# A float32 decoder trunk on one core: W-times-x products as three 256-column matmuls per tile instead of one of 512 and one of 256

## The chip, the cores and the metric

The kernel runs on one NeuronCore of a Trainium2 chip (trn2). The metric is the device time of one execution in microseconds (us), as a median over runs. TensorE (PE in the profile) does the matmuls; its weight loads are shown as an engine of their own, PEld. VectorE is DVE, ScalarE is ACT, GpSimd is POOL, and SyncE (SP) issues most DMAs.

## The reference

The reference is a two-layer decoder trunk on x of 256 tokens by 2048 channels, in float32. Layer 0 mixes retention (4 heads) with a gated linear recurrence; layer 1 is 16-head causal attention with a bias table. Each layer ends in a gated MLP with a width-3 depthwise convolution. Cut to the parts that load weights:

```python
def reference(x, ...):
    for l in range(2):
        hn = rmsnorm(x, norm_mix[l])
        y = even_mixer(hn, ev_w_in[0], ...) if l % 2 == 0 else odd_mixer(hn, od_w_in[0], ...)
        x = x + y                            # both mixers: (hn @ w_in) -> mix -> @ w_out
        x = x + conv_ffn(rmsnorm(x, norm_ffn[l]), ffn_w_up[l], ..., ffn_w_down[l])
    return x

def conv_ffn(h, w_up, conv_w, conv_b, w_down):       # w_up 2048 x 11264, w_down 5632 x 2048
    u = causal_dwconv(h @ w_up, conv_w, conv_b)
    gate, val = jnp.split(u, 2, axis=-1)
    return (jax.nn.gelu(gate) * val) @ w_down
```

## The kernel before

**Split operands.** TensorE reads its operands as fp32r. To keep float32 accuracy, each weight chunk W is split into w_hi (a rounded copy, made by ACT) and w_lo = W - w_hi (made by DVE), and each activation x is split in the same way; the tiles `xs` and `act` hold x_hi and x_lo side by side, 256 tokens each, so that one tile is 512 columns. A product is w_hi x_hi + w_hi x_lo + w_lo x_hi; the term w_lo x_lo is left out.

**Chunks.** Weights stream in chunks of 256 rows by 512 columns (512 KB) into a ring of four slots: SP issues the DMA into `raw`, ACT makes w_hi (`split`, L373), DVE makes w_lo (`split`, L958), and PE uses the chunk. A slot is written again when the semaphore `chunk_used` says that PE is through with it. Each of the three engines walks through the same list of chunks: 12 blocks of 8 chunks for the input projection, 4 blocks of 8 for w_out, 22 half-pairs of 8 for w_up, 4 blocks of 22 for w_down, and the same for layer 1. In between, at fixed chunks of a block (`stage` 0 to 7), ACT and DVE do the work on the previous block's result.

**Products with W loaded.** `chunk_products` (L660) takes two k-tiles (u) by four output tiles (m) of a chunk, so 8 tiles of 128 x 128 weights. For each it runs `hi`, 512 columns wide (w_hi against x_hi and x_lo at once, L675), and `lo`, 256 columns wide (w_lo against x_hi, L679). Two tiles are interleaved: hi, hi, lo, lo. An output tile has a PSUM bank of 512 columns: columns 0:256 hold w_hi x_hi + w_lo x_hi, and columns 256:512 hold w_hi x_lo, the cross half. Four banks make a group, and blocks alternate between the two groups. The last chunk of the program, `last_chunk` (L692), has the same matmuls with the m loop outside, and a signal for each m.

**Draining.** One engine operation can't add the two halves out of PSUM, so ACT first copies the cross half to the SBUF tile `cross` (`copy_cross`, L384), DVE adds the main half to it (`drain_normed`, L974), and multiplies by `rstd` (L976), with the semaphores `cross_copied`, `acc_drained` and `normed` between them. For w_out and w_down, DVE adds `cross` and then the main half to the residual x_res (`add_residual`, L990 and L992). At the end of the program DVE does the same, tile by tile, straight from PSUM (L1450, L1452), and SP stores each tile. Two blocks of layer 0 (5 and 8) use the same group as the block before them; they are drained in two halves (`HALVED`).

**Products with x loaded.** The v blocks of layer 0 and all input blocks of layer 1 load x as the stationary operand and stream W, in `chunk_values` (L708): three matmuls of 512 columns one after another into one bank. They are not touched by the change.

Of the kernel before, what the change touches and what calls it, by code (L numbers as in the profile page):

```python
# [85 lines left out]
class Phase:  # L86


    def __init__(self, layer):
# [10 lines left out]
        own_in = 10 if layer == 0 else 0  # L100
        self.cross_in = layer * (10 + OUTB + 2 * PAIRS + OUTB)
        self.cross_out = self.cross_in + own_in
        self.cross_up = self.cross_out + OUTB
        self.cross_down = self.cross_up + 2 * PAIRS
        self.normed_in = layer * (10 + 2 * PAIRS)
        self.normed_up = self.normed_in + own_in
# [21 lines left out]
def build(nc, x_t, params, w_gates, rope, decay, rel_bias, buckets, identity,  # L128
# [21 lines left out]
    cross, _ = place("cross", [P, BT, S])  # L150
# [64 lines left out]
    cross_copied, acc_drained, normed = sem("cross_copied"), sem("acc_drained"), sem("normed")  # L215
    cross_half, half_drained = sem("cross_half"), sem("half_drained")
# [139 lines left out]
    def _(eng):  # L356
# [18 lines left out]
        def copy_cross(n, used, group, halved=False):  # L375

            eng.wait_ge(chunk_used, used)
            if not (isinstance(n, int) and n == 0):
                eng.wait_ge(acc_drained, n)
            if halved:  # L380
                act_f(cross[:, 0:2, :], ps[:, 4 * group:4 * group + 2, S:2 * S], ACT.Copy).then_inc(cross_half, 1)
                act_f(cross[:, 2:4, :], ps[:, 4 * group + 2:4 * group + 4, S:2 * S], ACT.Copy).then_inc(cross_copied, 1)
            else:
                act_f(cross[:, :, :], ps[:, 4 * group:4 * group + 4, S:2 * S], ACT.Copy).then_inc(cross_copied, 1)  # L384

# [19 lines left out]
        def residual(stage, j, n, used, group, norm):  # L405
            if stage == 2:
                copy_cross(n, used, group)
# [8 lines left out]
        def mlp_post(stage, ph, half, j):  # L416
# [3 lines left out]
            if stage == 2:  # L420
                copy_cross(n, chunk_end(ph.q_up + 4 * j + 2 * half, KC - 1), half)
            if stage == 3:
                eng.wait_ge(normed, ph.normed_up + 2 * j + half + 1)
# [22 lines left out]
        def lru_conv_first(half):  # L446
            eng.wait_ge(normed, half + 1)
# [34 lines left out]
        def gelu_branch(half):  # L482
            eng.wait_ge(normed, 3 + half)
            act_f(gl_gelu[:, half * BT:(half + 1) * BT, :], h[:, :, :], ACT.Gelu_apprx_tanh).then_inc(gelu_gl, 1)

        def silu_gate(grp):
            eng.wait_ge(normed, (7, 10)[grp])
# [51 lines left out]
        def even_post(b, stage):  # L539

            ph = phases[0]
            if b and stage == drain_stage(EVEN_GROUPS, b) and EVEN_BLOCKS[b - 1][0] != "v":
# [966 lines left out]
```

## Time and profile before

| | us |
|---|---|
| median of 3 runs | 2249.24 (2248.87 to 2251.79) |
| the profiled execution, its own time | 2249.13 |
| its span in the trace | 2247.3 |
| PE busy | 2240.0 |
| PE weight loads busy | 1943.2 |
| DVE busy | 1494.7 |
| ACT busy | 1157.5 |

The span runs from the first to the last instruction of the core. "Busy" is the time covered by at least one instruction of the engine. Matmuls overlap each other, so the mean length of one (396 ns for 512 columns) is not what it costs in a stream; that is read from one start to the next. A row of a timeline that ends in "x2" merges two instructions, and its time is that of the first one's start.

### The profile page before, as it was taken

The numbers are of one execution on the slowest core, as the hardware profiler recorded it, in microseconds if no ns is written. First come the engines' busy times: TensorE is split into PE (matmuls) and PEld (weight loads), VectorE is DVE, ScalarE is ACT, GpSimd is POOL, SyncE is SP. The second block draws the span as 40 slices with busy tenths as digits, with TensorE's granted clock in tenths as the row PEclk, the third lists the DMA queues.
The fourth block names the chain that finished last, engine by engine and source line by source line (L and its number), as shares of the span: only waits on it lengthen the run. The fifth ranks groups of instructions, "written<-read, shape, count | busy, mean of one in ns | idle before, by whom it ended". The sixth has DMA issues, their size and how long they took to land.

```text
span 2247.3 us, 34057 instructions
## 1 busy us (share of the span) xinstructions
PE 2240.0 (100%) x12502; PEld 1943.2 (86%) x12502; DVE 1494.7 (67%) x1798; ACT 1157.5 (52%) x1451; POOL 7.2 (0%) x17
## 2 busy tenths in 40 slices
PE   9999999999999999999999999999999999999999
PEld 8888888888888888888888888888888888888888
DVE  7886766777677777544565656567777777774444
ACT  6654355555555555444455555555555555553333
POOL 0000000000000000000000000000000000000000
PEclk9999999999999999999999999999999999999999
DMA  8655655666666666666675555556665666566664
GB/s 273 182 178 164 192 176 184 185 189 190 189 188 187 196 179 193 189 185 192 197 224 169 167 180 168 169 179 188 187 197 178 192 187 197 178 196 200 200 187 143
DMA packets 216385, 420.90 MB, mean 187 GB/s; under 512 B 13061, under 2 KB 13589, under 8 KB 216176
## 3 DMA queue, kind: packets, MB, share of 16 engines
q1 hardware_dynamic: 214416, 413.59, 59.9%
q0 software_dynamic: 1456, 5.65, 0.7%
q8 instruction: 54, 0.88, 0.2%
q10 hardware_dynamic: 432, 0.56, 0.1%
q14 instruction: 27, 0.22, 0.0%
HBM read 417.62 MB, written 2.12 MB: 187 GB/s over the span
## 4 chain that ended last, share of the span: by engine, by line
PE 99%; DMA 0%; DVE 0%; ACT 0%; issue 0%; ACTq 0%; DVEq 0%
PE ps L675 56%; PE ps L679 28%; PE ps L718 5%; PE ps L720 5%; PE ps L719 5%; PE ps L757 0%; PE ps L801 0%; PE ps L812 0%; PE ps L739 0%; PE ps L758 0%; PE ps L820 0%; PE ps L751 0%; DMA x_res<-x_t 0%; PE ps L811 0%; PE ps L775 0%; PE ps L726 0%
## 5 line engine op out<-in xcount | busy, mean ns | idle before, releaser
L958 DVE TENSOR_TENSOR w_lo<-raw,w_hi 128x1024 fp32r<-128x1024 f32 x783 | 948.9, 1223 | 554.3 <-ACT w_hi L373 535.4
L373 ACT ACTIVATE w_hi<-raw 128x1024 fp32r<-128x1024 f32 x783 | 811.3, 1054 | 570.3 <-PE ps L679 491.1
L675 PE MATMUL ps<-xs,w_hi 128*128 128x512 f32 x3456 | 1086.5, 396 | 3.0 <-DVE w_lo L1387 2.9
L679 PEld LDWEIGHTS ps<-xs,w_lo 128*128 128x128 f32 x3456 | 649.2, 188 | 153.4
L679 PE MATMUL ps<-xs,w_lo 128*128 128x256 f32 x3456 | 678.9, 278 | 0.0
L675 PE MATMUL ps<-act,w_hi 128*128 128x512 f32 (+1 forms) x1912 | 600.8, 396 | 0.0
L675 PEld LDWEIGHTS ps<-xs,w_hi 128*128 128x128 f32 x3456 | 526.3, 189 | 4.1 <-DVE xs L1007 3.1
L679 PEld LDWEIGHTS ps<-act,w_lo 128*128 128x128 f32 x1912 | 359.2, 188 | 84.9
L679 PE MATMUL ps<-act,w_lo 128*128 128x256 f32 (+1 forms) x1912 | 375.6, 278 | 0.0
L675 PEld LDWEIGHTS ps<-act,w_hi 128*128 128x128 f32 x1912 | 291.1, 189 | 0.1
L718 PE MATMUL ps<-w_hi,xs 128*128 128x512 f32 x448 | 176.0, 393 | 0.0
L720 PE MATMUL ps<-w_hi,xs 128*128 128x512 f32 x448 | 174.4, 389 | 0.0
L719 PE MATMUL ps<-w_lo,xs 128*128 128x512 f32 x448 | 174.4, 389 | 0.0
L384 ACT ACTIVATE cross<-ps 128x1024 f32<-128x1024 f32 x67 | 68.8, 1027 | 112.7 <-PE ps L679 112.5
L974 DVE TENSOR_TENSOR h<-ps,cross 128x1024 f32<-128x1024 f32 x52 | 63.6, 1224 | 75.7 <-ACT cross L384 75.7
L720 PEld LDWEIGHTS ps<-w_hi,xs 128*128 128x128 f32 x448 | 84.1, 188 | 17.6
L719 PEld LDWEIGHTS ps<-w_lo,xs 128*128 128x128 f32 x448 | 84.2, 188 | 16.9
L718 PEld LDWEIGHTS ps<-w_hi,xs 128*128 128x128 f32 x448 | 84.1, 188 | 16.9
L427 ACT ACTIVATE buf_g<-h,par 128x256 f32<-128x256 f32 x88 | 45.8, 591 | 43.3 <-DVE h L976 43.3
L976 DVE TENSOR_TENSOR h<-h,rstd 128x1024 f32<-128x1024 f32 x54 | 66.1, 1225 | 2.0
L427 ACT ACTIVATE buf_v<-h,par 128x256 f32<-128x256 f32 x88 | 45.8, 591 | 40.2 <-DVE h L976 40.2
L431 ACT ACTIVATE buf_g<-buf_g 128x1024 f32<-128x1024 f32 x22 | 23.4, 1063 | 66.6 <-DVE buf_g L1076 66.6
(186 smaller groups left out, 813.4 us busy)
## 6 DMA issues: line engine op xcount, KB each, us to landing
raw<-w_up SPq DMA_DIRECT2D x352, 512.0 KB, 3.6
raw<-w_in SPq DMA_DIRECT2D x191, 512.0 KB, 4.1
raw<-w_down SPq DMA_DIRECT2D x176, 512.0 KB, 4.6
raw<-w_out SPq DMA_DIRECT2D x64, 512.0 KB, 4.8
bias<-bias_line POOLq DMA_DIRECT2D x1, 2048.0 KB, 11.3
x_res<-x_t SPq DMA_DIRECT2D x3, 512.0 KB, 7.3
out_t<-x_res POOLq DMA_DIRECT2D x3, 512.0 KB, 3.1
gates_w<-w_gates POOLq DMA_DIRECT2D x1, 1024.0 KB, 5.4
```

The lines of the kernel that those rows point to most:

```text
L373: act_f(w_hi[:, s, :, :], raw[:, s, :, :], ACT.Copy).then_inc(hi_ready, 1)
L384: act_f(cross[:, :, :], ps[:, 4 * group:4 * group + 4, S:2 * S], ACT.Copy).then_inc(cross_copied, 1)
L427: ins = act_f(buf[:, t, :], h[:, t, :], ACT.Identity, scale=w, bias=b)
L431: act_f(buf_g[:, :, :], buf_g[:, :, :], ACT.Gelu_apprx_tanh).then_inc(gelu_done, 1)
L675: return mm(ps[:, 4 * group + m, :], w_hi[:, s, u, m * P:(m + 1) * P], rhs, start=first and u == 0, stop=False)
L679: return mm(ps[:, 4 * group + m, 0:S], w_lo[:, s, u, m * P:(m + 1) * P], rhs[:, 0:S], start=False, stop=last and u == CT - 1)
L718: mm(out, x_hi, w_hi[:, s, u, :], start=first and u == 0, stop=False)
L719: mm(out, x_hi, w_lo[:, s, u, :], start=False, stop=False)
L720: ins = mm(out, x_lo, w_hi[:, s, u, :], start=False, stop=last and u == CT - 1)
L958: tt(w_lo[:, s, :, :], raw[:, s, :, :], w_hi[:, s, :, :].bitcast(F32), ALU.subtract).then_inc(lo_ready, 1)
L974: tt(dst, ps[:, 4 * group:4 * group + 4, 0:S], cross[:, :, :], ALU.add).then_inc(acc_drained, 1)
L976: tt(dst, dst, spread(rstd[:, 0:S], BT), ALU.mult).then_inc(normed, 1)
```

## The change

Every tile of a product with W loaded becomes three matmuls of 256 columns that all add into columns 0:256 of the bank: w_hi x_hi, w_hi x_lo, w_lo x_hi, in this order and without interleaving two tiles. The cross half in PSUM, the tile `cross`, the ACT copies and the DVE adds of the cross half go away with their semaphores. DVE drains by one multiplication of PSUM by `rstd`, and waits for `chunk_used` itself. What waited on `normed` now waits on `acc_drained`. Counts of matmuls with W loaded: 5376 tiles, before 5376 of 512 columns and 5376 of 256, after 16128 of 256. The columns streamed are the same, 768 a tile.

```diff
-                def hi(m):
-                    return mm(ps[:, 4 * group + m, :], w_hi[:, s, u, m * P:(m + 1) * P], rhs,
-                              start=first and u == 0, stop=False)
-
-                def lo(m):
-                    return mm(ps[:, 4 * group + m, 0:S], w_lo[:, s, u, m * P:(m + 1) * P], rhs[:, 0:S],
-                              start=False, stop=last and u == CT - 1)
-
-                for m in range(0, BT, 2):
+                for m in range(BT):
                     if drained is not None and (u, m) == (0, BT // 2):
 
                         pe.wait_ge(acc_drained, drained)
-                    hi(m)
-                    hi(m + 1)
-                    lo(m)
-                    ins = lo(m + 1)
+                    out, cols = ps[:, 4 * group + m, 0:S], slice(m * P, (m + 1) * P)
+                    mm(out, w_hi[:, s, u, cols], rhs[:, 0:S], start=first and u == 0, stop=False)
+                    mm(out, w_hi[:, s, u, cols], rhs[:, S:2 * S], start=False, stop=False)
+                    ins = mm(out, w_lo[:, s, u, cols], rhs[:, 0:S], start=False, stop=last and u == CT - 1)
             ins.then_inc(chunk_used, 1)
...
-        def drain_normed(n, n_cross, n_normed, group, dst, halved=None):
-
+        def drain_normed(n, used, group, dst, halved=None):
+
+            eng.wait_ge(chunk_used, used)
+            step.sync()
...
             else:
-                eng.wait_ge(cross_copied, n_cross)
-                step.sync()
-                tt(dst, ps[:, 4 * group:4 * group + 4, 0:S], cross[:, :, :], ALU.add).then_inc(acc_drained, 1)
+                tt(dst, ps[:, 4 * group:4 * group + 4, 0:S], spread(rstd[:, 0:S], BT), ALU.mult).then_inc(acc_drained, 1)
             eng.wait_ge(acc_drained, n + 1)
-            tt(dst, dst, spread(rstd[:, 0:S], BT), ALU.mult).then_inc(normed, 1)
-            eng.wait_ge(normed, n_normed)
...
-        def add_residual(j, n, n_cross, group):
-            eng.wait_ge(cross_copied, n_cross)
+        def add_residual(j, n, used, group):
+            eng.wait_ge(chunk_used, used)
             x = x_res[:, j * BT:(j + 1) * BT, :]
-            step.sync()
-            step(tt(x, x, cross[:, :, :], ALU.add))
             step.sync()
...
-            step(tt(x, x, ps[:, 4 + m, S:2 * S], ALU.add))
             step.sync()
             tt(x, x, ps[:, 4 + m, 0:S], ALU.add).then_inc(last_added, 1)
```

The first place is PE, the start of a chunk inside the w_up loop. Before (`xs` is the split activation, the last figures are rows by columns of the output):

```order
1414 L675 MATMUL ps<-xs,w_hi 128x512 [waits lo_ready]
1415 L675 MATMUL ps<-xs,w_hi 128x512
1416 L679 MATMUL ps<-xs,w_lo 128x256 x2
1417 L675 MATMUL ps<-xs,w_hi 128x512 x2
1418 L679 MATMUL ps<-xs,w_lo 128x256 x2
```

The same place after:

```order
3396 L653 MATMUL ps<-xs,w_hi 128x256 [waits lo_ready]
3397 L654 MATMUL ps<-xs,w_hi 128x256
3398 L655 MATMUL ps<-xs,w_lo 128x256
3399 L653 MATMUL ps<-xs,w_hi 128x256
3400 L654 MATMUL ps<-xs,w_hi 128x256
3401 L655 MATMUL ps<-xs,w_lo 128x256
```

Four matmuls for two tiles have become six, no two neighbours work on different tiles any more except where one tile ends, and the wait for the chunk stands at the first one as before.

The second place is DVE in the first block after the start, where it drains block 0. Before:

```order
39 L958 TENSOR_TENSOR w_lo<-raw,w_hi 128x1024 [waits hi_ready,rstd_ready]
40 L974 TENSOR_TENSOR h<-ps,cross 128x1024 [waits dve_step,cross_copied]
41 L976 TENSOR_TENSOR h<-h,rstd 128x1024 [waits acc_drained]
42 L958 TENSOR_TENSOR w_lo<-raw,w_hi 128x1024 [waits hi_ready,normed]
43 L1105 TENSOR_SCALAR small<-par 128x8
```

The same place after:

```order
38 L1016 SCALAR_TENSOR_TENSOR rstd<-rstd,h 128x258 [waits dve_step]
39 L923 TENSOR_TENSOR w_lo<-raw,w_hi 128x1024 [waits hi_ready,rstd_ready]
40 L936 TENSOR_TENSOR h<-ps,rstd 128x1024 [waits dve_step,chunk_used]
41 L923 TENSOR_TENSOR w_lo<-raw,w_hi 128x1024 [waits hi_ready,acc_drained]
42 L1063 TENSOR_SCALAR small<-par 128x8
```

Two operations have become one, and the one that is left waits for PE itself and no longer for ACT's copy. On ACT the row of L384 between two splits is gone in the same way.

## Rows read from the trace of the kernel before

**Rows 1.** The page, parts 1 and 2: busy us (share) xinstructions; granted TensorE clock.
```profile
PE 2240.0 (100%) x12502; PEld 1943.2 (86%) x12502; DVE 1494.7 (67%) x1798; ACT 1157.5 (52%) x1451; POOL 7.2 (0%) x17
...
PEclk9999999999999999999999999999999999999999
```

**Rows 2.** The page, part 4: the chain that ended last, by line.
```profile
PE ps L675 56%; PE ps L679 28%; PE ps L718 5%; PE ps L720 5%; PE ps L719 5%; PE ps L757 0%; PE ps L801 0%; PE ps L812 0%; PE ps L739 0%; PE ps L758 0%; PE ps L820 0%; PE ps L751 0%; DMA x_res<-x_t 0%; PE ps L811 0%; PE ps L775 0%; PE ps L726 0%
```

**Rows 3.** Waits of PE: us in total, times, longest.
```profile
PE ps L675 <- DVE w_lo L1387: 2.9, 1, 2.9
PE ps L854 <- POOL ones L327: 1.0, 1, 1.0
```

**Rows 4.** Waits, all engines: who waited for whom, us, times, longest.
```profile
DVE w_lo L958 <- ACT w_hi L373: 535.4, 355, 8.1
ACT w_hi L373 <- PE ps L679: 491.1, 334, 4.4
```

**Rows 5.** Groups of PE: busy us, mean ns | idle before.
```profile
L675 PE MATMUL ps<-xs,w_hi 128*128 128x512 f32 x3456 | 1086.5, 396 | 3.0 <-DVE w_lo L1387 2.9
L679 PE MATMUL ps<-xs,w_lo 128*128 128x256 f32 x3456 | 678.9, 278 | 0.0
L675 PE MATMUL ps<-act,w_hi 128*128 128x512 f32 (+1 forms) x1912 | 600.8, 396 | 0.0
L679 PE MATMUL ps<-act,w_lo 128*128 128x256 f32 (+1 forms) x1912 | 375.6, 278 | 0.0
...
L704 PE MATMUL ps<-act,w_lo 128*128 128x256 f32 x8 | 1.6, 278 | 0.0
```

**Rows 6.** Timeline of PE in the w_up loop, near 700 and near 729 us.
```profile
700.13 0.40 PE L679 MATMUL ps<-xs,w_lo 128*128 128x256 f32 x2
700.37 0.63 PE L675 MATMUL ps<-xs,w_hi 128*128 128x512 f32 x2
700.84 0.39 PE L679 MATMUL ps<-xs,w_lo 128*128 128x256 f32 x2
701.06 0.62 PE L675 MATMUL ps<-xs,w_hi 128*128 128x512 f32 x2
...
729.39 0.40 PE L679 MATMUL ps<-xs,w_lo 128*128 128x256 f32 x2
```

**Rows 7.** Windows of MLP stages: us, busy (x) by engine, PEclk, DMA share, GB/s.
```profile
700.00:900.00 200.00, 200.00 (x1150) 174.52 (x1149) 148.80 (x172) 108.56 (x127) 0.00 (x0) 1.00 0.61 187
```

**Rows 8.** Timeline of PE where eight 256-column fp32r matmuls follow each other.
```profile
217.69 0.28 PE L775 MATMUL ps<-sq_hi,ones_r 128*128 128x256 f32 x1
217.81 0.28 PE L775 MATMUL ps<-sq_lo,ones_r 128*128 128x256 f32 x1
217.93 0.28 PE L775 MATMUL ps<-sq_hi,ones_r 128*128 128x256 f32 x1
...
218.65 0.63 PE L675 MATMUL ps<-xs,w_hi 128*128 128x512 f32 x2
```

**Rows 9.** Timeline of PE in a block with x loaded, 19 starts apart.
```profile
1179.68 0.39 PE L719 MATMUL ps<-w_lo,xs 128*128 128x512 f32 x1
...
1183.99 0.39 PE L720 MATMUL ps<-w_hi,xs 128*128 128x512 f32 x1
```

**Rows 10.** The chain in order of time: start us, us, what; transposes of 128 columns.
```profile
1161.73 0.88 PE ps L801 x8
...
1215.11 1.31 PE ps L820 x12
```

**Rows 11.** Weight loads that repeat the operand just loaded, by line: L775's forms.
```profile
L775 PEld LDWEIGHTS ps<-sq_hi,ones_r x8: 187/192/192, 217.6 to 290.9; 128*128 128x128 f32 x8
L775 PEld LDWEIGHTS ps<-sq_lo,ones_r x8: 192/192/192, 217.7 to 291.0; 128*128 128x128 f32 x8
```

**Rows 12.** Groups of ACT and DVE that the change removes or alters.
```profile
L384 ACT ACTIVATE cross<-ps 128x1024 f32<-128x1024 f32 x67 | 68.8, 1027 | 112.7 <-PE ps L679 112.5
L976 DVE TENSOR_TENSOR h<-h,rstd 128x1024 f32<-128x1024 f32 x54 | 66.1, 1225 | 2.0
L974 DVE TENSOR_TENSOR h<-ps,cross 128x1024 f32<-128x1024 f32 x52 | 63.6, 1224 | 75.7 <-ACT cross L384 75.7
L990 DVE TENSOR_TENSOR x_res<-x_res,cross 128x1024 f32<-128x1024 f32 x15 | 18.4, 1226 | 22.0 <-ACT cross L384 22.0
```

**Rows 13.** Timeline of all engines at the end of the span.
```profile
2243.57 0.41 DVE L1450 TENSOR_TENSOR x_res<-x_res,ps 128x256 f32<-128x256 f32 x1
2243.64 0.40 PE L704 MATMUL ps<-act,w_lo 128*128 128x256 f32 x2
2244.02 0.42 DVE L1452 TENSOR_TENSOR x_res<-x_res,ps 128x256 f32<-128x256 f32 x1
2244.36 0.41 DVE L1450 TENSOR_TENSOR x_res<-x_res,ps 128x256 f32<-128x256 f32 x1
2244.80 0.42 DVE L1452 TENSOR_TENSOR x_res<-x_res,ps 128x256 f32<-128x256 f32 x1
```

**Rows 14.** Timeline of PE inside the w_down loop, 36 rounds apart.
```profile
900.08 0.39 PE L679 MATMUL ps<-act,w_lo 128*128 x2
...
925.16 0.39 PE L679 MATMUL ps<-act,w_lo 128*128 x2
```

More of the change, by code:

```diff
@@ L373, in split @@
             act_f(w_hi[:, s, :, :], raw[:, s, :, :], ACT.Copy).then_inc(hi_ready, 1)
[L375 to L384, printed above, removed]
         def split_x(j, norm):
@@ L419, in mlp_post @@
             buf = buf_v if half else buf_g
-            if stage == 2:
-                copy_cross(n, chunk_end(ph.q_up + 4 * j + 2 * half, KC - 1), half)
             if stage == 3:
-                eng.wait_ge(normed, ph.normed_up + 2 * j + half + 1)
+                eng.wait_ge(acc_drained, n + 1)
                 for t in range(BT):
@@ L446, in lru_conv_first @@
         def lru_conv_first(half):
-            eng.wait_ge(normed, half + 1)
+            eng.wait_ge(acc_drained, half + 1)
             for t in range(BT):
@@ L541, in even_post @@
             ph = phases[0]
-            if b and stage == drain_stage(EVEN_GROUPS, b) and EVEN_BLOCKS[b - 1][0] != "v":
-                copy_cross(b - 1, RING * (ph.q_in + 2 * b), EVEN_GROUPS[b - 1], (0, b) in HALVED)
             if b in (1, 2) and stage == 3:
@@ L700, in last_chunk @@
                 for u in range(CT):
-                    rhs = src[:, kt + u, :, :].rearrange("p a s -> p (a s)")
-                    mm(ps[:, 4 * group + m, :], w_hi[:, s, u, cols], rhs, start=False, stop=False)
-                for u in range(CT):
-                    ins = mm(ps[:, 4 * group + m, 0:S], w_lo[:, s, u, cols], src[:, kt + u, 0, :],
-                             start=False, stop=u == CT - 1)
+                    out = ps[:, 4 * group + m, 0:S]
+                    mm(out, w_hi[:, s, u, cols], src[:, kt + u, 0, :], start=False, stop=False)
+                    mm(out, w_hi[:, s, u, cols], src[:, kt + u, 1, :], start=False, stop=False)
+                    ins = mm(out, w_lo[:, s, u, cols], src[:, kt + u, 0, :], start=False, stop=u == CT - 1)
                 ins.then_inc(tail_done, 1)
@@ L1031, in sum_squares, with residual @@
                 eng.wait_ge(ss_ready, norm + 1)
-        def residual(stage, j, n, n_cross, group, norm):
+        def residual(stage, j, n, used, group, norm):
             if stage == 2:
-                add_residual(j, n, n_cross, group)
+                add_residual(j, n, used, group)
             if stage == 4 and norm is not None:
@@ L1064, in mlp_post @@
             if stage == 2:
-                drain_normed(n, ph.cross_up + 2 * j + half + 1, ph.normed_up + 2 * j + half + 1, half, h[:, :, :])
+                drain_normed(n, chunk_end(ph.q_up + 4 * j + 2 * half, KC - 1), half, h[:, :, :])
             if stage == 4:
@@ L1259, in even_post @@
                 else:
-                    values_before = sum(x[0] == "v" for x in EVEN_BLOCKS[:b])
                     h_free(b)
-                    drain_normed(b - 1, b - values_before, b - values_before, EVEN_GROUPS[b - 1], h[:, :, :], (0, b))
+                    drain_normed(b - 1, RING * (ph.q_in + 2 * b), EVEN_GROUPS[b - 1], h[:, :, :], (0, b))
             if b in (1, 2) and stage in (4, 5, 6):
@@ L1399, in _ @@
                     if b == 0 and l:
-                        residual(c, 3, phases[0].n_down + 3, ph.cross_in, 1, 2)
+                        residual(c, 3, phases[0].n_down + 3, RING * ph.q_in, 1, 2)
                     post(b, c)
@@ L1439, in _ @@
                     else:
[L1440 removed]
+                        residual(c, b - 1, ph.n_down + b - 1, RING * ph.q_down + FC * b, (b - 1) % 2, None if l else 2)
                 with eng.Fori(*DOWN_TURNS) as t:
```

31 lines of the change are left out of this document (8 added, 23 removed).

## The prediction

> **What bounds the kernel now.** Start with the page's busy times: PE is busy 2240.0 of 2247.3 us, at 9 tenths or more of the clock in every slice (1.00 in the window of [rows 7]), while DVE has 67% and ACT 52% [rows 1]. A busy share alone proves little, so the next view is the chain that ended last: the products with W loaded hold 56% (L675) and 28% (L679) of the span, the three lines of the values blocks 15%, and no other engine a whole per cent [rows 2]. The list of waits confirms it from the other side: PE was held up twice, for 3.9 us together, both times in the start-up [rows 3]. And the helpers run on PE's leash: ACT's split waits 491.1 us for PE to give ring slots back, DVE's split waits 535.4 us for ACT [rows 4]. So the time of this kernel is the sum of what PE's instructions cost in a stream, plus a few us at both ends. Anything that the change takes from ACT and DVE is worth nothing unless PE waits for it; anything that it adds to each PE tile is paid 5376 times (3456 + 1912 + 8 of the 256-column form [rows 5]).
>
> **What a tile costs before.** Not 396 + 278 ns, the lengths of the two matmuls, since matmuls overlap. I take starts: from the lo pair at 700.13 to the lo pair at 729.39 us there are 42 rounds of hi, hi, lo, lo, so 29.26 / 42 = 0.6967 us a round and 348.3 ns a tile [rows 6]. It is the pace of the whole stage, since a window of 200 us counts 1150 matmuls, 174 ns each, two a tile [rows 7].
>
> **What a tile costs after.** Three matmuls of 256 columns, each with its own weight load, all adding into one bank. The trace of before has this form in one place, the column sums of the retention norm (L775): fp32r, 256 columns, a load each, four in a row into one PSUM range, with the moving operand alternating between two tiles. Eight of them take from 217.69 to 218.65 us, 120 ns each [rows 8]. Three make 360.0 ns. The difference is 360.0 - 348.3 = 11.7 ns a tile, times 5376 tiles: +62.9 us.
>
> Why should the same 768 columns take longer? Set the rows beside the full clock of 2.4 GHz, at which 256 columns are 106.7 ns and 512 are 213.3 ns. The values blocks with 512 columns step by (1183.99 - 1179.68) / 19 = 226.8 ns [rows 9], which is 13.5 ns above the columns; L775 is 13.3 ns above; a round of four in the products is 696.7 - 640 = 56.7 ns above, 14.2 ns a matmul. So a matmul with its load costs its columns plus some 13 to 14 ns whatever its width, and the change buys a third one for each tile.
>
> **Bounds of that price.** The row that speaks for less is in the products themselves: from a lo pair's start to the next hi pair's are 0.24 us once and 0.22 us once, so about 115 ns a matmul [rows 6]. Three at this price would be 345 ns, 3.3 less than now: -18 us. But the hi matmuls beside them step by 0.233 (0.47 from 700.37 to 700.84 for two), above the 226.8 of a pure stream of 512, so what the lo ones save in the mixture the hi ones pay; only a round's sum can be relied on. The row for more: if a 512-column matmul costs 226.8 [rows 9], the round leaves (696.7 - 453.6) / 2 = 121.5 ns for a 256-column one, so 364.5 ns a tile, +87 us. Between -18 and +87 I take +62.9, since L775 is the same instruction in the same succession; read to 10 ns over eight steps it is good to 1.2 ns a matmul, so +44 to +82 from this row alone.
>
> **Same bank three times.** Before, neighbours mostly write different banks. L775 and the values blocks (three in a row to one bank) show no stall for it beyond the 13 ns. Costed at nothing, it is in the 120.
>
> **Weight loads.** They are hidden now and stay hidden, but with less to hide behind: a load and a transpose of 128 columns step by 1.31 / 12 = 109 ns [rows 10], where the columns alone are 53, so the load needs at most 109 ns. A 256-column matmul of 120 ns covers that by 11 ns. The second w_hi load of a tile is redundant, but nothing drops it: L775 loads `ones_r` anew for each of 16 matmuls [rows 11].
>
> **A rule of the Trainium skill.** L775's 120 ns and the values' 226.8 ns stand 13 ns above their columns [rows 8, 9]. The Trainium skill, "TensorE: Matmul & The Clock Gate", section "Wait — 56ns, not 53.3ns?", gives a fixed cost of about 2.5 ns for each warm matmul. By that rule an estimate for the change would be 5376 x 2.5 = +13 us, about 2262; the rows here are five times as large, and the sum goes by them.
>
> **ACT and DVE.** What goes: 67 copies of the cross half on ACT, 68.8 us; one of the two drain operations on DVE, 66.1 us; 15 adds to the residual, 18.4 us [rows 12]. The drain that stays reads PSUM and writes h like the 1224 ns add before it, so I give it the same length. What hides all of this now is PE itself; a block is drained while the other PSUM group fills, 8 chunks or over 22 us later. In the two blocks without a second group (5 and 8 of layer 0), PE first has the gate products or the retention values to do, and no PE wait shows there today [rows 3]. Worth on the path: 0; were that cover gone, the path to PE would be one halved multiplication instead of a halved copy and a halved add, still no more than now. The new wait is DVE's own on `chunk_used`, before which it waited for ACT, which waited for the same signal; behind it in DVE's queue stand the w_lo splits, and they come earlier than now by a copy's 1.03 us. Nothing is moved past a DMA queue. The transfers (0.61 of the DMA engines in the MLP [rows 7]) are asked for at PE's pace, so a slower PE only relaxes them.
>
> **The ends.** After the last matmul DVE now does L1450 and L1452, then the store [rows 13]. L1450 goes: -0.4 us. At the start PE waits for the first weights as before; some 0.1 us of the eight first tiles' extra is hidden there.
>
> **Sum**, against the profiled execution's own time of 2249.13 us, 0.1 below the median of the runs: 2249.1 + 62.9 - 0.4 - 0.1 = 2311.5, say 2312 us, 2.8% slower.
>
> **Rivals.** *First, no charge for the split of 512.* The cost would go by columns: hi 233, lo 115 ns looks just like two to one [rows 6], and 768 columns stay 348.3 ns. The same would come out if the 13 ns belonged to a change of weights and the second w_hi load were dropped after all (the change then not doing what it says). Time 2249.1 - 0.5 = 2248.6 us, say 2249; with a charge of 1 to 3 ns for each further matmul instead of none, 5 to 16 us more, 2254 to 2265. Against it: the 13 ns above the columns at both widths [rows 8, 9] and the repeated loads of [rows 11]. Chance 0.05, of which 0.04 for no charge and 0.01 for the small one. The small charge is what the rule of the Trainium skill above amounts to.
>
> *Second, the faster side.* A 256-column matmul in this stream costs the 115 ns of L679 because the shorter one can follow any predecessor at that pace, and the hi matmuls' extra belongs to 512-column moving operands. It decides from 116.1 ns down (348.3 / 3); at 115 it gives 2249 - 18 - 0.5 = 2231 us. For it: thousands of L679 against sixteen L775. Against it: L775 has no 512 beside it, just as the new stream. Chance 0.06.
>
> *Third, PE's instruction supply becomes the limit.* Today PE must be given a load and a matmul each 174 ns [rows 7]; after, each 120 ns, and in the w_down loop one more register instruction for each k-tile. The eight L775 and the twelve transposes at 109 ns [rows 10] are short enough to have been queued up before. Each ns above 120 would cost 16128 x 1 ns = 16 us; at 124 it is 2376. Nothing in the rows shows a pace it couldn't hold, and the w_down loop with its register instructions keeps the same round, (925.16 - 900.08) / 36 = 0.6967 us [rows 14]. The same price would fall due if the loads needed more than 120 ns, which the 109 excludes. Chance 0.06.
>
> **How the numbers follow.** My forecast, 13 ns for each further matmul: 0.83, with 2312 us as its time and 2292 (118.8 ns, +44) to 2336 (121.5 ns, +87) as its own range. This is the range I give: the three others, 0.17, lie outside. A measurement of this kernel can tell about 0.2% from no change. Faster by more: the second rival, 0.06. Within 0.2%: the first with no charge, 0.04. Slower by more: the forecast, the third, and the first with its small charge, 0.83 + 0.06 + 0.01 = 0.90.
>
> **What would show it.** Starts in the w_up loop: 120 ns each in an even beat, 360 a tile. If they alternate around 116, the second rival holds; if the beat is above 122 or PE shows gaps in the w_down loop only, the third. PE's chain share stays 99%, its count goes from 12502 to 17878, as do the weight loads. DVE should fall by some 85 us and ACT by some 69, and the waits of ACT's split for PE grow. If PE shows waits for DVE at block starts, my zero for the drains is wrong. If PE's clock drops below the full one anywhere, all of the above is off.

## The result

| | before | after |
|---|---|---|
| median, us | 2250.51 (2248.87 to 2252.04) | 2310.78 (2310.62 to 2311.22) |
| the profiled execution, us | 2249.13 | 2310.62 |
| its span, us | 2247.3 | 2308.8 |

The ratio is 1.0271, 95% interval 1.0259 to 1.0283: 2.7% slower. The prediction was 2312 us with a range of 2292 to 2336.

The page of the changed kernel, parts 1 and 4, beside [rows 1, 2]:

```profile
PE 2303.8 (100%) x17878; PEld 2245.8 (97%) x17878; DVE 1414.3 (61%) x1725; ACT 1110.0 (48%) x1380; POOL 7.2 (0%) x17
...
PE ps L653 28%; PE ps L655 28%; PE ps L654 28%; PE ps L683 4%; PE ps L685 4%; PE ps L684 4%; PE ps L722 0%; PE ps L766 0%; PE ps L777 0%; PE ps L704 0%; PE ps L723 0%; PE ps L785 0%; PE ps L716 0%; DMA x_res<-x_t 0%; PE ps L776 0%; PE ps L740 0%
```

PE has 5376 matmuls more and is again busy all the time. The three lines of a tile share the chain equally, 28% each, where before it was 56% and 28%. PEld went from 86% of the span to 97%: a load's row is some 190 ns long and the loads now start 120 ns apart, so their rows overlap. Helpers have become idler: DVE fell by 80 us, ACT by 48.

The timeline of PE in the w_up loop, beside [rows 6]:

```profile
700.16 0.28 PE L655 MATMUL ps<-xs,w_lo 128*128 128x256 f32 x1
700.28 0.28 PE L653 MATMUL ps<-xs,w_hi 128*128 128x256 f32 x1
700.40 0.28 PE L654 MATMUL ps<-xs,w_hi 128*128 128x256 f32 x1
...
736.16 0.28 PE L655 MATMUL ps<-xs,w_lo 128*128 128x256 f32 x1
```

The beat is even, 0.12 us from start to start. Between the first and the last row lie 36.00 us and 100 tiles, so 360 ns a tile. Before it was 348.3. That is the whole result to within 1.4 us: 11.7 ns x 5376 tiles = 62.9 us, where the span grew by 61.5.

The waits of PE, and the longest ones of the helpers, beside [rows 3, 4]:

```profile
PE ps L653 <- DVE w_lo L1344: 1.4, 1, 1.4
PE ps L819 <- POOL ones L318: 1.0, 1, 1.0
...
ACT w_hi L364 <- PE ps L655: 914.9, 556, 5.3
DVE w_lo L923 <- ACT w_hi L364: 736.7, 454, 8.4
DVE h L936 <- PE ps L655: 28.5, 44, 0.7
```

PE still waits for nobody after the start-up. ACT's wait for PE before a split nearly doubled, from 491 to 915 us. Of these 424 us, 48 are work that is gone and 62 are the longer span; 112.5 had been the wait for PE before the cross copies [rows 12], and some 174 had been ACT's waits for DVE in the MLP (the lines L427, L431 and L435 had 213.7 us of them before, the same operations 39.8 after). So most of it is waiting that has moved. The last row is the new wait of the drain; it costs nothing, as no wait of PE stands behind it.

The end of the span, DVE alone, beside [rows 13]:

```profile
2305.58 0.42 DVE L1408 TENSOR_TENSOR x_res<-x_res,ps 128x256 f32<-128x256 f32 x1 [0.30 <-PE ps L670]
2306.30 0.42 DVE L1408 TENSOR_TENSOR x_res<-x_res,ps 128x256 f32<-128x256 f32 x1 [0.29 <-PE ps L670]
```

One add per tile is left, and DVE now waits 0.3 us for each instead of running behind. The last matmul of the kernel starts at 2305.98 (0.32 us before the add), and the span ends 2.8 us later. Before, it started at 2243.76 (the second of the pair at 2243.64) and the span ended 3.5 us later. The gain at the end is 0.7 us.

### The profile page after: what moved, and what is told of

Read it like the earlier page. It is cut to its first block, busy times and chain, and to the rows that moved or that the text cites. A ratio compares the mean times of both kernels' runs of the same rounds, so it can differ in the third digit from the quotient of the medians.

```text
span 2308.8 us, 44731 instructions
## 1 busy us (share of the span) xinstructions
PE 2303.8 (100%) x17878; PEld 2245.8 (97%) x17878; DVE 1414.3 (61%) x1725; ACT 1110.0 (48%) x1380; POOL 7.2 (0%) x17
## 4 chain that ended last, share of the span: by engine, by line
PE 100%; DMA 0%; DVE 0%; ACT 0%; ACTq 0%; issue 0%; DVEq 0%
PE ps L653 28%; PE ps L655 28%; PE ps L654 28%; PE ps L683 4%; PE ps L685 4%; PE ps L684 4%; PE ps L722 0%; PE ps L766 0%; PE ps L777 0%; PE ps L704 0%; PE ps L723 0%; PE ps L785 0%; PE ps L716 0%; DMA x_res<-x_t 0%; PE ps L776 0%; PE ps L740 0%
## 5 line engine op out<-in xcount | busy, mean ns | idle before, releaser
L923 DVE TENSOR_TENSOR w_lo<-raw,w_hi 128x1024 fp32r<-128x1024 f32 x783 | 954.3, 1223 | 752.1 <-ACT w_hi L364 736.7
L364 ACT ACTIVATE w_hi<-raw 128x1024 fp32r<-128x1024 f32 x783 | 823.6, 1057 | 995.2 <-PE ps L655 914.9
L653 PE MATMUL ps<-xs,w_hi 128*128 128x256 f32 x3456 | 979.3, 283 | 1.4 <-DVE w_lo L1344 1.4
L655 PE MATMUL ps<-xs,w_lo 128*128 128x256 f32 x3456 | 978.1, 283 | 0.0
L654 PE MATMUL ps<-xs,w_hi 128*128 128x256 f32 x3456 | 978.1, 283 | 0.0
L653 PEld LDWEIGHTS ps<-xs,w_hi 128*128 128x128 f32 x3456 | 663.5, 192 | 2.3 <-DVE xs L965 1.6
L654 PEld LDWEIGHTS ps<-xs,w_hi 128*128 128x128 f32 x3456 | 663.5, 192 | 0.1
L655 PEld LDWEIGHTS ps<-xs,w_lo 128*128 128x128 f32 x3456 | 663.5, 192 | 0.0
L653 PE MATMUL ps<-act,w_hi 128*128 128x256 f32 (+1 forms) x1912 | 541.5, 283 | 0.0
L655 PE MATMUL ps<-act,w_lo 128*128 128x256 f32 (+1 forms) x1912 | 541.1, 283 | 0.0
L654 PE MATMUL ps<-act,w_hi 128*128 128x256 f32 (+1 forms) x1912 | 541.1, 283 | 0.0
L654 PEld LDWEIGHTS ps<-act,w_hi 128*128 128x128 f32 x1912 | 367.1, 192 | 0.0
L653 PEld LDWEIGHTS ps<-act,w_hi 128*128 128x128 f32 x1912 | 367.1, 192 | 0.0
L655 PEld LDWEIGHTS ps<-act,w_lo 128*128 128x128 f32 x1912 | 367.1, 192 | 0.0
L936 DVE TENSOR_TENSOR h<-ps,rstd 128x1024 f32<-128x1024 f32 x52 | 63.6, 1223 | 28.5 <-PE ps L655 28.5
L403 ACT ACTIVATE buf_g<-h,par 128x256 f32<-128x256 f32 x88 | 45.8, 592 | 14.2 <-DVE h L936 14.2
```

The source lines that it names most:

```text
L364: act_f(w_hi[:, s, :, :], raw[:, s, :, :], ACT.Copy).then_inc(hi_ready, 1)
L403: ins = act_f(buf[:, t, :], h[:, t, :], ACT.Identity, scale=w, bias=b)
L653: mm(out, w_hi[:, s, u, cols], rhs[:, 0:S], start=first and u == 0, stop=False)
L654: mm(out, w_hi[:, s, u, cols], rhs[:, S:2 * S], start=False, stop=False)
L655: ins = mm(out, w_lo[:, s, u, cols], rhs[:, 0:S], start=False, stop=last and u == CT - 1)
L923: tt(w_lo[:, s, :, :], raw[:, s, :, :], w_hi[:, s, :, :].bitcast(F32), ALU.subtract).then_inc(lo_ready, 1)
```

## Experiments

The theory on trial: a matmul with its weight load costs its columns at 2.4 GHz plus about 13 ns, whatever the width, and the drains are worth nothing. All ratios are against the kernel before, measured beside it on the same chip.

### Is it the three adds into one bank?

```diff
-                for m in range(BT):
+                for m in range(0, BT, 2):
...
-                    out, cols = ps[:, 4 * group + m, 0:S], slice(m * P, (m + 1) * P)
-                    mm(out, w_hi[:, s, u, cols], rhs[:, 0:S], start=first and u == 0, stop=False)
-                    mm(out, w_hi[:, s, u, cols], rhs[:, S:2 * S], start=False, stop=False)
-                    ins = mm(out, w_lo[:, s, u, cols], rhs[:, 0:S], start=False, stop=last and u == CT - 1)
+                    for k in (m, m + 1):
+                        mm(ps[:, 4 * group + k, 0:S], w_hi[:, s, u, k * P:(k + 1) * P], rhs[:, 0:S],
+                           start=first and u == 0, stop=False)
+                    for k in (m, m + 1):
+                        mm(ps[:, 4 * group + k, 0:S], w_hi[:, s, u, k * P:(k + 1) * P], rhs[:, S:2 * S],
+                           start=False, stop=False)
+                    for k in (m, m + 1):
+                        ins = mm(ps[:, 4 * group + k, 0:S], w_lo[:, s, u, k * P:(k + 1) * P], rhs[:, 0:S],
+                                 start=False, stop=last and u == CT - 1)
```

> The changed kernel, but the three matmuls of two neighbouring tiles are interleaved (w_hi x_hi of both, w_hi x_lo of both, w_lo x_hi of both), so that neighbours in the stream always add into different PSUM banks. Fixed charge for each matmul with its load (13.3 ns beside its columns, my theory): nothing changes, starts 120 ns apart, 2311 us. Same-bank theory (the 12 ns a tile come from adding three times in a row into one range): most of the 61 us come back, a tile near 348 ns, 2250 to 2260 us.

Measured: 2311.18 us, ratio 1.0274 (1.0257 to 1.0291), the same as the changed kernel. Its timeline of PE, where x2 merges the two tiles:

```profile
719.90 0.40 PE L653 MATMUL ps<-xs,w_hi 128*128 128x256 f32 x2
720.14 0.40 PE L656 MATMUL ps<-xs,w_hi 128*128 128x256 f32 x2
720.38 0.40 PE L659 MATMUL ps<-xs,w_lo 128*128 128x256 f32 x2
```

0.24 us a pair, 120 ns a matmul, with another bank each time. The same-bank theory falls. In this order w_hi of one tile is no longer loaded twice in a row either, and that changes nothing.

### The two halves of the change, each alone

The matmul half. The hi matmul of the kernel before is issued as two, into the same places:

```diff
-                    return mm(ps[:, 4 * group + m, :], w_hi[:, s, u, m * P:(m + 1) * P], rhs,
-                              start=first and u == 0, stop=False)
+                    for part in (slice(0, S), slice(S, 2 * S)):
+                        mm(ps[:, 4 * group + m, part], w_hi[:, s, u, m * P:(m + 1) * P], rhs[:, part],
+                           start=first and u == 0 and part.start == 0, stop=False)
```

> The kernel before, with one edit: the 512-column matmul is issued as two of 256 columns, the second into the cross half of the bank as before, so that ACT's copies and DVE's adds of the cross half are all still there. It is the matmul half of the change alone. Fixed charge for each matmul: 120 ns a start, 360 ns a tile, 2249 + 63 = 2312 us, at most 1 us above the changed kernel, whose end is 0.4 us shorter. If taking the helpers' work away had brought something that the matmuls then lost: above 2315 us. Same-bank theory: also a loss here, since both halves lie in one bank, so this run is no test of it.

Measured: 2312.68 us, ratio 1.028 (1.0263 to 1.0297), with all copies and adds of the cross half in place.

The drain half. The changed kernel takes back the matmuls of before (the last chunk's too, not shown):

```diff
...
-                    mm(out, w_hi[:, s, u, cols], rhs[:, 0:S], start=first and u == 0, stop=False)
-                    mm(out, w_hi[:, s, u, cols], rhs[:, S:2 * S], start=False, stop=False)
-                    ins = mm(out, w_lo[:, s, u, cols], rhs[:, 0:S], start=False, stop=last and u == CT - 1)
...
+                    hi(m)
+                    hi(m + 1)
+                    lo(m)
+                    ins = lo(m + 1)
```

> The changed kernel with the matmuls of before (512 and 256 columns, hi, hi, lo, lo): the cross half is computed and then left out of every sum, so the term w_hi x_lo is missing from the result. It is the drain half of the change alone: no copies of the cross half on ACT, one DVE operation a drain, no second add to the residual. Fixed charge, and helpers hidden behind TensorE: 2249 - 0.4 = 2249 us, within 1 us of before. If the helpers' work costs TensorE anything now (ring slots handed over late, SBUF or PSUM shared with the copies): below 2245 us.

Measured: 2248.93 us, ratio 0.9996 (0.9986 to 1.0005). Its page has the helpers' load of the changed kernel and the PE of before:

```profile
PE 2242.1 (100%) x12502; PEld 1945.2 (87%) x12502; DVE 1414.5 (63%) x1725; ACT 1110.3 (49%) x1380; POOL 7.2 (0%) x17
```

80 us less DVE and 47 us less ACT bought nothing that can be measured. The two halves add up: about 63 us from the matmuls, 0 from the drains, and the two together are the changed kernel.

### Half the dose

```diff
-                    return mm(ps[:, 4 * group + m, :], w_hi[:, s, u, m * P:(m + 1) * P], rhs,
-                              start=first and u == 0, stop=False)
+                    for part in (slice(0, S), slice(S, 2 * S)) if u == 0 else (slice(0, 2 * S),):
+                        mm(ps[:, 4 * group + m, part], w_hi[:, s, u, m * P:(m + 1) * P], rhs[:, part],
+                           start=first and u == 0 and part.start == 0, stop=False)
```

> Half the dose of the split: as the kernel before, but the hi matmul is issued as two of 256 columns in the first k-tile of each chunk only (u = 0), and as one of 512 in the second. 2688 matmuls more than before, where the whole split has 5376. Fixed charge for each matmul: half of the 63 us, 2281 us. If the order of widths has a price of its own, as the runs with four and four (+13 us) and alternating (+24 us) say, up to half of such an amount more, 2281 to 2292 us.

Measured: 2280.83 us, ratio 1.0141 (1.0125 to 1.0158). The medians are 31.8 us apart (2280.83 - 2248.99) for 2688 matmuls more, 11.8 ns each; the whole split has 63.5 us (2312.68 - 2249.21) for 5376, 11.8 ns each. The price is by the matmul.

### The charge at other widths

Wider, where the load is well hidden. First the hi matmul of the kernel before with 384 columns:

```diff
-                    return mm(ps[:, 4 * group + m, :], w_hi[:, s, u, m * P:(m + 1) * P], rhs,
-                              start=first and u == 0, stop=False)
+                    n = 2 * S if first and u == 0 else S + P
+                    return mm(ps[:, 4 * group + m, 0:n], w_hi[:, s, u, m * P:(m + 1) * P], rhs[:, 0:n],
+                              start=first and u == 0, stop=False)
```

> The kernel before with 384 columns instead of 512 in the hi matmul (save the ones that start a sum), so half of the term w_hi x_lo is left out. The load is hidden at this width. Columns plus a fixed charge: a round 106.7 ns shorter, 5096 tiles x 53.3 ns = 272 us less, 1977 us, and 14 ns a matmul over the columns as before. If the charge grew with the columns (the first rival of the prediction), the 128 columns would take 58 ns with them, 296 us less, 1953 us. VectorE (1495 us) and ACT (1158 us) stay below both.

Then the lo matmul of the kernel before with 512:

```diff
-                    return mm(ps[:, 4 * group + m, 0:S], w_lo[:, s, u, m * P:(m + 1) * P], rhs[:, 0:S],
+                    return mm(ps[:, 4 * group + m, :], w_lo[:, s, u, m * P:(m + 1) * P], rhs,
                               start=False, stop=last and u == CT - 1)
```

> The kernel before with the lo matmul as wide as the hi one, 512 columns (it adds w_lo x_lo, which the other kernels leave out, into the cross half). Every matmul of the kernel's stream is then 512 wide, in the order hi, hi, lo, lo. Open question: before, hi matmuls step by 233 ns and lo ones by 115, while even streams step by 227 and 120. If that comes from mixing the widths: 227 ns a matmul as in the blocks with x loaded, a tile 454 ns, 2249 + 5376 x 0.105 = 2815 us. If it belongs to these operands (W stationary, xs or act moving): 233 ns, a tile 466 ns, 2882 us.

With 512 everywhere: 2813.54 us, ratio 1.2508 (1.2483 to 1.2533), 1.5 us from the forecast of the mixing theory. Its timeline in the w_up loop:

```profile
725.90 0.62 PE L679 MATMUL ps<-xs,w_lo 128*128 128x512 f32 x2
...
746.75 0.62 PE L679 MATMUL ps<-xs,w_lo 128*128 128x512 f32 x2
```

Between the rows are 23 rounds of four in 20.85 us, 226.6 ns a matmul, 13.3 above the columns. So these operands have the same price as those of [rows 9]; the 233 and 115 ns of [rows 6] come from having both widths in one stream.

With 384: 2016.15 us, ratio 0.8959 (0.8943 to 0.8976). The pace was as forecast and the total was not, as its timeline and then the waits of PE and of its weight loads show:

```profile
715.49 0.40 PE L680 MATMUL ps<-xs,w_lo 128*128 128x256 f32 x2
...
729.57 0.40 PE L680 MATMUL ps<-xs,w_lo 128*128 128x256 f32 x2
```

```profile
PEld ps L676 <- DVE w_lo L959: 30.5, 73, 2.0
PE ps L676 <- DVE w_lo L959: 12.9, 28, 1.8
```

24 rounds of two 384- and two 256-column matmuls in 14.08 us are 587 ns a round, 53 above the 533 of the columns, again 13.3 a matmul. But 2016 is 39 us over the forecast. PE now waits for w_lo in places, and its loads do so for 30.5 us together, in rows that did not exist before; PE is busy 1991.5 of 2014.5 us. How much of the 39 us these waits make is not worked out. DVE now holds 26% of the chain that ended last and ACT 8%. At a chunk of 2.35 us (four rounds) the helpers are no longer free. That is the point where the drains of the change could be worth something; this was not tried. It need not be the only thing that holds there: ACT's splits waited 168 us for the DMAs of the weights, 11 in the kernel before.

Narrower, where the load can't hide. The changed kernel with 128 columns of x_lo:

```diff
-                    mm(out, w_hi[:, s, u, cols], rhs[:, S:2 * S], start=False, stop=False)
+                    mm(out[:, 0:P], w_hi[:, s, u, cols], rhs[:, S:S + P], start=False, stop=False)
```

> The changed kernel, but the second matmul of each tile streams only the first 128 columns of x_lo, so half of the term w_hi x_lo is left out. Columns plus a fixed charge: a step of 53.3 + 13.3 = 67 ns for it, a tile 307 ns, 2311 - 5376 x 0.0533 = 2024 us. Load-bound theory (a step can't be shorter than the weight load, at most 109 ns by the transposes): a tile of 120 + 120 + 109 = 349 ns, 2311 - 59 = 2252 us; if the load's floor is the 120 ns itself, nothing changes, 2311 us. In the load-bound cases the charge is a matter of the load and not of the width.

And with all three matmuls of the changed kernel at 128 columns:

```diff
-                    mm(out, w_hi[:, s, u, cols], rhs[:, 0:S], start=first and u == 0, stop=False)
-                    mm(out, w_hi[:, s, u, cols], rhs[:, S:2 * S], start=False, stop=False)
-                    ins = mm(out, w_lo[:, s, u, cols], rhs[:, 0:S], start=False, stop=last and u == CT - 1)
+                    n = S if first and u == 0 else P
+                    mm(out[:, 0:n], w_hi[:, s, u, cols], rhs[:, 0:n], start=first and u == 0, stop=False)
+                    mm(out[:, 0:P], w_hi[:, s, u, cols], rhs[:, S:S + P], start=False, stop=False)
+                    ins = mm(out[:, 0:P], w_lo[:, s, u, cols], rhs[:, 0:P], start=False, stop=last and u == CT - 1)
```

> The changed kernel, but all three matmuls of a tile stream 128 columns instead of 256 (save the ones that start a sum), so the sums of the tokens 128 to 255 are left out almost everywhere. It shows the floor that the weight load alone sets. If a load takes 109 ns and the 120 ns of the 256-column stream is columns plus a fixed charge, starts are 109 ns apart, a tile 327 ns, 2311 - (5096 x 0.033 = 168) = 2143 us. If the 120 ns is already the load's own cycle, 120 ns, 2311 us. If neither binds, 67 ns a matmul, and TensorE would wait for VectorE and the DMAs well below 1900 us.

With half of the cross term left out: 2251.83 us, ratio 1.0011 (1.0001 to 1.0022). Columns plus 13 ns would have given 2024; the load's floor gave 2252. Its timelines of PE and of the loads:

```profile
720.27 0.22 PE L654 MATMUL ps<-xs,w_hi 128*128 128x128 f32 x1
720.33 0.33 PE L655 MATMUL ps<-xs,w_lo 128*128 128x256 f32 x1
720.50 0.28 PE L653 MATMUL ps<-xs,w_hi 128*128 128x256 f32 x1
720.62 0.22 PE L654 MATMUL ps<-xs,w_hi 128*128 128x128 f32 x1
```

```profile
720.15 0.19 PEld L654 LDWEIGHTS ps<-xs,w_hi 128*128 128x128 f32 x1
720.27 0.19 PEld L655 LDWEIGHTS ps<-xs,w_lo 128*128 128x128 f32 x1
720.38 0.19 PEld L653 LDWEIGHTS ps<-xs,w_hi 128*128 128x128 f32 x1
720.50 0.19 PEld L654 LDWEIGHTS ps<-xs,w_hi 128*128 128x128 f32 x1
```

The matmul behind the narrow one has its start recorded 60 ns after it, at 720.33, but the next one starts only at 720.50. The likely reading, which no row states, is that its weights, which began to load at 720.27, were not there yet. A tile is 0.35 us, as long as in the kernel before, with 128 columns fewer. The loads follow each other by 120, 110 and 120 ns, never closer.

With 128 columns everywhere: 2226.17 us, ratio 0.9893 (0.9875 to 0.9911), though little more than half of the columns are left. The first timeline shows the floor; the windows (us, busy and count of PE, PEld, DVE, ACT, POOL, then the granted clock, DMA share, GB/s) and the timeline of the start show why it isn't the 2143 that was expected:

```profile
724.79 0.27 PE L654 MATMUL ps<-xs,w_hi 128*128 128x128 f32 x1
...
735.85 0.27 PE L654 MATMUL ps<-xs,w_hi 128*128 128x128 f32 x1
```

```profile
0.00:56.00 56.00, 53.76 (x252) 51.96 (x252) 28.89 (x43) 28.14 (x42) 4.41 (x13) 0.59 0.62 222
56.00:111.00 55.00, 55.00 (x254) 54.40 (x254) 22.46 (x51) 14.37 (x16) 0.00 (x0) 0.51 0.32 95
```

```profile
10.62 0.41 PE L654 MATMUL ps<-xs,w_hi 128*128 128x128 f32 x1
10.83 0.42 PE L655 MATMUL ps<-xs,w_hi 128*128 128x128 f32 x1
...
107.35 4.78 PE L705 MATMUL ps<-xc,gates_w 128*128 128x256 f32 x16
```

99 matmuls take 11.06 us, 112 ns each, not 109: 335 ns a tile, so 5096 x 25 ns = 127 us less than the changed kernel, 2183. The 280 tiles that start a sum are shorter as well, 0.34 us (680.18 to 680.52) for 0.36, some 5 us more. The other 43 to 48 us lie in the first 112 us, where the clock fell to the 1.2 GHz level. It was granted in full while PE ran its first matmuls from 8.56 us on. It fell at about 10.6 us, in the midst of a stream of 128-column matmuls, from where on they start 0.21 us apart, and it was full again from about 112 us, behind the 16 gate matmuls of 256 columns. In between, 465 matmuls of all widths took 101 us, as long as 800 right afterwards, and PE was not idle once. The gate matmuls start at 107.35 us here and at 65.26 us in the changed kernel: 42 us lost by then.

The 1.2 GHz level also says what kind of floor this is. From 103.94 to 107.14 us 15 matmuls of 128 columns take 213 ns each, where the columns alone are 107. A limit by which PE were given its instructions at a fixed pace, the third rival of the prediction, would have stayed near 112 ns; this one goes with TensorE's clock, as a load inside TensorE would. That it is the load is the likely reading; no run changes the load alone.

Seven other traces have that level too, but for 3 to 7 us and not for 100: the clock is at 0.50 from somewhere between 8 and 11 us on, soon after PE's wait for the first w_lo, in the runs with 128 columns of x_lo, the drains alone, 384, 512, the swapped order, four and four, and alternating. With 384 columns it is there a second time, from about 119 to 125 us, behind a wait of 1.8 us for w_lo. The other six, the kernels before and after among them, don't have it, though PE waits in the same place. The scatter between runs of one kernel goes with it: those of the kernel before at a mean clock of 1.000 took 2248.5 to 2250.0 us, those at 0.998 2251.7 to 2252.3.

### What mixing the widths costs

Three other orders of the same 16 matmuls of a chunk of the kernel before, and one that swaps only the banks. Four and four:

```diff
-                for m in range(0, BT, 2):
+                for m in range(BT):
...
                     hi(m)
-                    hi(m + 1)
-                    lo(m)
-                    ins = lo(m + 1)
+                for m in range(BT):
+                    ins = lo(m)
```

> The kernel before with another order of the same matmuls: hi of four tiles, then lo of the four. The stream of before pays 56.7 ns over its columns in a round of four, 3.4 more than four times the 13.3 of an even stream. Theory that this is the price of changing the width (two changes a round, 1.7 ns each): half of the changes go, 1344 x 3.4 = 4.6 us, 2245 us. Rival, that it is a matter of 512-column matmuls as such: nothing changes, 2249 us.

Alternating:

```diff
-                for m in range(0, BT, 2):
+                for m in range(BT):
...
                     hi(m)
-                    hi(m + 1)
-                    lo(m)
-                    ins = lo(m + 1)
+                    ins = lo(m)
```

> The kernel before with hi, lo, hi, lo: twice the changes of width, and each lo adds into the bank of the hi just before it. Width-change theory: 2688 x 3.4 = 9 us more, 2258 us. Rival, no price for the order and none for adding twice in a row into one bank: 2249 us. A weight load starts when the matmul before it starts; if the load for a hi, which has only a 256-column lo to hide behind, comes late, it does so once a tile in both orders, so this says nothing on loads.

Eight and eight, with the first k-tile's hi, the second's hi, and then the lo matmuls in the same order:

```diff
             for u in range(CT):
...
+                for m in range(BT):
...
+                    mm(ps[:, 4 * group + m, :], w_hi[:, s, u, m * P:(m + 1) * P], rhs[u],
+                       start=first and u == 0, stop=False)
+            for u in range(CT):
+                for m in range(BT):
+                    ins = mm(ps[:, 4 * group + m, 0:S], w_lo[:, s, u, m * P:(m + 1) * P], rhs[u][:, 0:S],
+                             start=False, stop=last and u == CT - 1)
```

> The kernel before with all eight hi matmuls of a chunk first and then all eight lo. Runs of one width are twice as long as with four and four. If only the first few matmuls of a run step slower than in an even stream, the loss against even streams shrinks again: half of what four and four has over 13.4 ns a matmul (2.3 of 15.7), 10752 x 1.2 = 12 us less than 2263, 2250 us, and still longer runs would beat before. If mixing costs the same however long the runs: 2263 us. If it goes on rising with the length (-, +13 us from two to four): 2270 us or more.

The banks of the lo matmuls swapped:

```diff
                     hi(m + 1)
-                    lo(m)
-                    ins = lo(m + 1)
+                    lo(m + 1)
+                    ins = lo(m)
```

> The kernel before, with the two lo matmuls of a round swapped: hi(m), hi(m+1), lo(m+1), lo(m). The widths come in the same order as before, but the first lo now adds into the bank of the hi just before it, as in the alternating run. If the alternating run's +24 us came from adding twice in a row into one bank, a part of it shows here: half of the tiles, +12 us, 2261 us. If it came from the order of widths alone: no change, 2249 us.

| order of widths | us | ratio | ns a matmul over its columns, w_up loop |
|---|---|---|---|
| one width only (after) | 2310.78 | 1.0271 (1.0259 to 1.0283) | 13.3 |
| one width only (all 512) | 2813.54 | 1.2508 (1.2483 to 1.2533) | 13.3 |
| hi hi lo lo (before) | 2249 to 2251 | 1 | 14.2 |
| the same, lo swapped | 2250.05 | 1.0000 (0.9991 to 1.001) | 14.2 |
| 8 hi, 8 lo | 2253.77 | 1.0018 (1.0009 to 1.0027) | 14.7 |
| 4 hi, 4 lo | 2262.73 | 1.0055 (1.0041 to 1.0069) | 15.3 |
| hi lo hi lo | 2274.38 | 1.0104 (1.0089 to 1.012) | 16.7 |

The last column is worked out from timelines such as these, of four and four, of eight and eight, and of the alternating order (in this sequence); over 5 to 6 us a reading is good to some 0.3 ns. That of the swapped order is from 172 rounds, 560.48 to 680.31 us, 696.7 ns each.

```profile
725.47 1.09 PE L675 MATMUL ps<-xs,w_hi 128*128 128x512 f32 x4
...
731.08 1.09 PE L675 MATMUL ps<-xs,w_hi 128*128 128x512 f32 x4
```

```profile
725.16 2.00 PE L677 MATMUL ps<-xs,w_hi 128*128 128x512 f32 x8
...
730.75 1.55 PE L677 MATMUL ps<-xs,w_hi 128*128 128x512 f32 x6
```

```profile
725.52 0.28 PE L679 MATMUL ps<-xs,w_lo 128*128 128x256 f32 x1
...
731.88 0.28 PE L679 MATMUL ps<-xs,w_lo 128*128 128x256 f32 x1
```

Four rounds of eight matmuls in 5.61 us are 1402 ns, 122 above the columns' 1280. Two rounds of sixteen in 5.59 us are 2795 each, 235 above 2560. Eighteen pairs in 6.36 us are 353.3 ns each, 33.3 above 320.

The width-change theory falls: four and four has half the changes of before and is slower. A price of banks falls too, since the swapped order is the same as before to 0.1%. What stands is that a stream of 512 and 256 columns has a price of its own, 1 to 3 ns a matmul beyond the 13.3, that it depends on the order, and that it neither rises nor falls evenly with the length of the runs (1, 2, 4, 8: +3.4, +0.9, +2.0, +1.4). In the mixture of 384 and 256 columns it isn't there. Why stays open.

The start of the alternating trace, at the 1.2 GHz level, adds one thing:

```profile
9.76 0.63 PE L675 MATMUL ps<-xs,w_hi 128*128 128x512 f32 x1
...
14.88 0.46 PE L675 MATMUL ps<-xs,w_hi 128*128 128x512 f32 x1
```

Eight pairs in 5.12 us are 640 ns each, which is 768 columns at 1.2 GHz and nothing over, where at the full clock the same pair has 33 ns over. The run with 512 everywhere steps by 428 ns at that level (9.72 to 12.29 us, six matmuls), where the columns are 427. So both the 13.3 ns and the price of the order belong to the full clock. Whether the 13.3 ns belong to the matmul or to its load, no run separates: every matmul of these kernels has a load of its own.

None of these orders beats the kernel before, and nothing in the runs points to a version that would: its own order is the cheapest of those tried with these matmuls, and the drains bring nothing while PE is the bound.

## Why the prediction was right, point by point

- **PE's stream is the time.** Right. The chain and the waits of PE are as before, and both halves of the change behave as that says: 0 for 80 us of DVE work, 63 us for 5376 matmuls.
- **A tile before, 348.3 ns, and after, 360.0.** Right to the reading: 36.00 us for 100 tiles. The eight matmuls of [rows 8] were the right precedent; thousands now step as they did.
- **A fixed 13 to 14 ns beside the columns.** Right for even streams of 256 and of 512 columns and for the mixture of 384 and 256 (13.3 each time), at the full clock. Wrong as "whatever its width": at 128 columns there is a floor, 112 ns a matmul, 59 above the columns. Wrong also for the mixture of 512 and 256 in other orders than that of before, 14.7 to 16.7. The forecast did not need those cases, since it took both prices, 348.3 and 360.0, from rows of the stream in question.
- **The bounds.** The lower end, 115 ns from the lo pairs, was a property of the mixture, as argued: once the neighbours are of one width, 256 costs 120 and 512 costs 227. The upper end, 121.5 ns, took the whole of the mixture's surplus for the 256-column one and was too high for the same reason.
- **Weight loads hidden, with 11 ns to spare.** Right in effect, but the margin was smaller: the floor of a load in this stream is 112 ns and not the 109 of the transposes, so 8 ns. The transposes were a near row and not the same one: their loads' rows last 141 ns, those of the products 192. The run with 128 columns everywhere shows it; PEld's 97% does not, as its rows overlap at any step below 190 ns.
- **Small charge.** The measured charge is 13.3 ns in even streams of 256 and of 512 columns. The estimate of 2262 us from the 2.5 ns of the Trainium skill, "TensorE: Matmul & The Clock Gate", section "Wait — 56ns, not 53.3ns?", was off by 49 us; the trace does not agree with it for fp32r matmuls that each load their weights.
- **Rivals.** No charge (2249) and the faster side (2231) did not come. Nor did a limit of instruction supply: the w_down loop, with its extra register instruction, keeps the beat, as its timeline in the changed kernel shows:

```profile
923.97 0.28 PE L654 MATMUL ps<-act,w_hi 128*128 128x256 f32 x1
...
940.16 0.28 PE L654 MATMUL ps<-act,w_hi 128*128 x1
```

These are 45 tiles in 16.19 us, 360 ns each.

- **ACT and DVE.** Forecast -69 and -85 us of busy time, measured -47.5 and -80.4. The operations went as counted, but the busy time of the splits that stay grew: L373's group had 811.3 us, L364's has 823.6, and L958's 948.9 became 954.3, though the mean split is only 3 ns longer on ACT and no longer on DVE. That is 12 of the 21 us by which ACT's figure is off; the other 9 are not accounted for. It is off the path, and the run with the drains alone shows the same busy times at the time of before.
- **The ends.** -0.7 us at the end instead of -0.4, because DVE had also been running behind its own second adds.

The sum against the spans: 62.9 - 0.7 - 0.1 = 62.1 forecast with the measured end, 61.5 measured. The 0.6 us that are left are 0.1 ns a tile, about what 10 ns over 100 tiles can tell.

## What to carry to other kernels

When TensorE is the bound and never waits, count matmuls as well as columns: here each fp32r matmul with its weight load cost 13.3 ns beside its columns, so cutting 512 columns into two of 256 cost 12 ns each time, and work saved on other engines pays for none of it as long as they wait for TensorE. At 128 columns a matmul still cost 112 ns, 8 ns less than at 256 with half of the columns, so narrowing one below 256 brings next to nothing. For a price that is to be multiplied by thousands, look for a stretch of the trace with the same instruction in the same company, however short, rather than take the mean of that instruction in other company.

## What was not expected of the hardware

- A stream of 512 and 256 columns costs more than the sum of even streams, by an amount that depends on the order: 0.9 ns a matmul in pairs, 3.4 ns when alternating. Between the two orders lie 24 us, 1% of this kernel. At the 1.2 GHz level the alternating stream cost its columns and nothing more.
- With 128-column matmuls the granted clock fell from 1.00 to 0.50 at about 10.6 us and stayed there until about 112 us, though PE was never idle in between; with 256 columns from the start it was at 1.00 throughout.
- A matmul's recorded start can be too early to read a step from: behind a 128-column one the start stood 60 ns after its predecessor's, and the delay showed only in the start after that, 0.17 us later. Only whole tiles or rounds can be relied on.
